# Moving the column sums and the spread of three norm passages to the last two steps of the tile loop

## The reference

```python
def rmsnorm_2(x, w):
    xf = x.astype(jnp.float32)
    y = xf * lax.rsqrt(jnp.mean(xf * xf, axis=-1, keepdims=True) + EPS)
    return (y * w.astype(jnp.float32)).astype(x.dtype)
...
        x = x + rmsnorm_2(y, norm_mix_post[layer])
        h = rmsnorm_2(x, norm_ffn_pre[layer])
        y = conv_ffn(h, ffn_w_up[layer], ffn_conv_w[layer], ffn_conv_b[layer], ffn_w_down[layer])
        x = x + rmsnorm_2(y, norm_ffn_post[layer])
        if layer == N_A_LAYERS - 1:
            k_sh, v_sh, c_sh = shared_kv(x, kv_norm, kv_w, kv_b_f)
```

## Time and profile before

| | |
|---|---|
| median of three runs | 2106.36 us (2105.05 to 2107.86) |
| time of the profiled execution | 2106.26 us |
| span in its profile | 2104.5 us |
| PE busy | 2046.5 us, 97% of the span |
| DVE busy | 1227.9 us, 58% |
| ACT busy | 791.7 us, 38% |
| mean granted clock of TensorE | 0.991 |

### The profile page before, as it was taken

One profiled execution on the slowest core, in us unless ns is written; L12 is line 12 of the kernel. 1 busy time (PEld: TensorE's weight loads), 2 busy tenths in 40 slices (PEclk: granted clock), 3 DMA queues, 4 the chain that ended last, 5 costly groups with the idle time before them and its releaser, 6 DMA issues.

```text
span 2104.5 us, 25495 instructions
## 1 busy us (share of the span) xinstructions
PE 2046.5 (97%) x9840; PEld 1658.8 (79%) x9848; DVE 1227.9 (58%) x1726; ACT 791.7 (38%) x1228; POOL 24.4 (1%) x45
## 2 busy tenths in 40 slices
PE   8999999999999999999899999999999999999997
PEld 6866778888888888877788888878786678888886
DVE  5778635454435355456675573774537767647475
ACT  4258243332222232245443342342426734324242
POOL 1000000000000000000000000000000000000000
PEclk9999999999999999999999999999999999999998
DMA  5410412322222222321122222222221022222221
GB/s 190 161 41 9 144 39 100 110 100 100 98 85 98 100 100 89 111 91 49 72 100 100 88 92 100 85 95 90 97 86 38 15 87 80 100 100 100 98 85 58
DMA packets 34320, 188.52 MB, mean 90 GB/s; under 512 B 4392, under 2 KB 8648, under 8 KB 14608
## 3 DMA queue, kind: packets, MB, share of 16 engines
q1 hardware_dynamic: 32448, 181.24, 24.2%
q0 software_dynamic: 1568, 5.65, 1.0%
q10 hardware_dynamic: 208, 0.33, 0.1%
HBM read 182.54 MB, written 2.11 MB: 88 GB/s over the span
## 4 chain that ended last, share of the span: by engine, by line
PE 86%; DVE 6%; PEld 3%; issue 2%; ACT 2%; DVEq 1%; PEldq 0%; DMA 0%; SPq 0%; ACTq 0%
PE bank L427 23%; PE bank L429 23%; PE bank L428 23%; PE bank L510 3%; PE bank L515 3%; PE bank L511 3%; PE bank L1242 2%; PE bank L1212 1%; PE bank L1229 1%; PEld bank L427 1%; PEld bank L429 1%; PEld bank L428 1%; PE bank L2250 1%; DVE xT L903 1%; DVE a_lo L688 1%
## 5 line engine op out<-in xcount | busy, mean ns | idle before, releaser
L356 ACT ACTIVATE w_hi<-w_raw 128x2048 fp32r<-128x2048 f32 (+3 forms) x168 | 307.7, 1832 | 760.6 <-PE bank L429 626.5
L427 PE MATMUL bank<-a_hi,w_hi 128*128 128x512 f32 x1376 | 538.6, 391 | 1.6 <-DVE w_lo L371 1.1
L429 PE MATMUL bank<-a_hi,w_lo 128*128 128x512 f32 x1376 | 535.6, 389 | 0.0
L428 PE MATMUL bank<-a_lo,w_hi 128*128 128x512 f32 x1376 | 535.5, 389 | 0.0
L371 DVE TENSOR_TENSOR w_lo<-w_raw,w_hi 128x2048 fp32r<-128x2048 f32 (+3 forms) x168 | 367.9, 2190 | 155.0 <-ACT w_hi L356 155.0
L427 PEld LDWEIGHTS bank<-a_hi,w_hi 128*128 128x128 f32 x1376 | 258.3, 188 | 56.5 <-issue 1.9
L429 PEld LDWEIGHTS bank<-a_hi,w_lo 128*128 128x128 f32 x1376 | 258.3, 188 | 53.8
L428 PEld LDWEIGHTS bank<-a_lo,w_hi 128*128 128x128 f32 x1376 | 258.4, 188 | 52.9
L427 PE MATMUL bank<-big_halves,w_hi 128*128 128x512 f32 x616 | 240.1, 390 | 0.5 <-DVE w_lo L371 0.3
L429 PE MATMUL bank<-big_halves,w_lo 128*128 128x512 f32 x616 | 239.7, 389 | 0.0
L428 PE MATMUL bank<-big_halves,w_hi 128*128 128x512 f32 x616 | 239.7, 389 | 0.0
(11 more groups left out here) (350 smaller groups left out, 2436.2 us busy)
## 6 DMA issues: line engine op xcount, KB each, us to landing
w_raw<-in_w_fu SPq DMA_DIRECT2D x44, 1024.0 KB, 4.8
w_raw<-in_w_up SPq DMA_DIRECT2D x16, 1024.0 KB, 4.8
w_raw<-in_w_down SPq DMA_DIRECT2D x16, 1024.0 KB, 4.8
w_raw<-in_w_fd SPq DMA_DIRECT2D x16, 1024.0 KB, 4.8
w_raw<-in_w_fd SPq DMA_DIRECT2D x8, 768.0 KB, 4.2
w_raw<-in_w_rqk SPq DMA_DIRECT2D x4, 1024.0 KB, 5.2
w_raw<-in_w_rvg SPq DMA_DIRECT2D x4, 1024.0 KB, 4.8
w_raw<-in_w_gate SPq DMA_DIRECT2D x4, 1024.0 KB, 4.8
```

Source lines behind the costliest of these rows:

```text
L356: act.activation(dst[0][:, cols], raw[slot][:, cols], ACT.Copy).then_inc(hi_half_ready.sem if half == 0 else hi_ready.sem, 1)
L427: pe.matmul(out, w[0], x[0], start=first, stop=False)
L428: pe.matmul(out, w[0], x[1], start=False, stop=False)
L429: return pe.matmul(out, w[1], x[0], start=False, stop=last)
```

## The change

The column sums stand after the eighth step instead of the sixth, and the spread after the ninth instead of the seventh. The instructions and their number are the same, and so are the instructions of the other engines and their order.

```diff
             def with_tile(pe, k):
-                if k == 5:
+                if k == 7:
                     pe.wait_ge(gathered.sem, b_ga + KT - 1)
                     column_sums(pe, 4, total, True, True).then_inc(sums_ready.sem, 1)
-                elif k == 6:
+                elif k == 8:
                     pe_root(pe)
```

## The result

The changed kernel takes 2116.2 us (median of five, 2115.4 to 2117.7) against 2106.4 us before (five, 2103.8 to 2107.9). The ratio is 1.0050, with a 95% interval of 1.0036 to 1.0064. That is 9.8 us slower by the medians; the forecast said 4.7.

A forecast was written before the change was run, and what follows sets the result against it. The prediction took PE as the bound, losing time where it waits or runs slower. Passage terms -0.85, +1.33 and +1.31 gave +1.8 us, two clock falls +2.9, so 2106.3 + 4.7 = 2111.0 us, range 2107.0 to 2113.6.

The forecast's parts named there:

- The wait at the sums: PE's wait for DVE's last additions before the column sums goes, returning 1.84, 0.98 and 1.25 us, 4.07 in all.
- the root's way: From sums to spread, root and reciprocal stay hidden under 2.37 us of sums and ninth step, with 0.77 us to spare.
- the third block waits for the first evacuation: With the spread last before it, PE's third block begins 3.22 us after the spread's start; PE stands 2.4 us.
- 11.04: Forecast time in us from the end of the sixth step to the third block, each passage, at full clock.
- the fourth block: In the feed-forward passages it waits 0.31 us more for the low weights that DVE splits.
- The terms of the second and the third passage: Net cost at full clock: +1.33 us in the second, +1.31 in the third including the fourth block's weight wait.
- the term of -0.85 us for the first passage: Net gain at full clock: 11.04 us against 12.20 now, -1.16, plus 0.31 for the fourth block's weights.
- the chance of a fall: Chance that the clock falls after each new wait: about 0.7; two falls taken, some 2.9 us.
- Case B: Rival: the clock falls behind the new wait in all three passages, 6.3 us slower, 2112.6 us; chance 0.22.
- C: Rival: third block waits, but the clock falls in one passage or none, 2108.1 to 2109.6 us; chance 0.28.
- D: Rival: the third block doesn't pay, the new wait much shorter than worked out; 2100.5 or 2105.8 us; chance 0.05.
- E: Rival: root's way not covered, ACT or DVE answering later; up to 0.6 us a passage, up to 2114.4; chance 0.03.

The follow-up runs named there:

- second profiles: Both kernels profiled and timed once more with no edit: the kernel before 2106.3 us, ratio 1.0001; the changed kernel 2115.4 us, ratio 1.0044.
- filled run: Changed kernel with nine more matmuls of 512 columns behind each spread, into a bank that nothing reads: 2113.4 us, ratio 1.0033 to the kernel before.
- second profile of before: The kernel before, profiled and timed once more with no edit: 2106.3 us, ratio 1.0001.

## Why the forecast was wrong

**Right: the mechanism and its place.** The wait at the sums went; the root's way is hidden; the third block waits for the first evacuation. 10.97 to 10.99 us from the sixth step in all three passages against 11.04; a wait of 2.2 us against 2.0 to 2.5; the fourth block 0.5 us late at full clock against 0.3. The terms of the second and the third passage, +1.33 and +1.31 us, came to 1.0 and 1.6 us in the second profiles (the stretch, and the fourth block's wait as in the filled run): 2.6 together, as forecast.

**Wrong, the step that failed most: the term of -0.85 us for the first passage.** It compared 11.04 with 12.20 us, of which 1.7 were a fall of the clock that the second profile of before hasn't. There the first passage's stretch is 27.0 us, as in the others, and the change costs it 1.2 us, with the fourth block's wait 1.7: the term was 2.6 us too low. The forecast noted the fall and counted its going as a gain. That the total of that execution matched the median was luck: a fall at 145 us and part of the slow stretch ahead of the first passage, both in the second profile, are missing from it.

**Wrong: the chance of a fall.** 0.7 a passage, two of three, 2.9 us. It was six of six in two profiles, and three falls cost 4.0 us by the comparison with the filled run (5.2 with the fourth block's wait in it). Case B, all three falls at 2112.6, was the better one. Its price for the falls, 4.5 us, was high enough; it was short by the term above and the one below.

**Missing: the clock ahead of a passage.** The forecast put it at nothing. Ahead of the second passage it fell 3 us earlier relative to the work, 1.2 us in the second profile; with the other entries and what lies ahead of the first one that is 0.9 us. The forecast also measured from the end of the sixth step, and so could not see what its +1.3 us a passage are made of. The old wait at the sums took up the slow first steps: the stretch is 27.0 us with 4 to 5 us of slow clock in them and 27.1 with none. The new order pays for them: 28.1 us with them, 26.8 without, so that with a full clock there the stretch would even have gained a little over 27.0.

With the terms set right the account is 3.16 + 5.17 + 1.40 - 0.53 = 9.20 us for the second profiles, against 9.8 by the medians of the first measurement and 9.2 by those of the second. The forecast's 4.7 lacks 4.5 of these 9.2: rounded, 2.6 us in the first passage's term, 1.1 in the falls and 0.9 ahead of the passages.

Of the rivals, C (the clock stays) fell; D fell with the waits of 2.2 us; E fell: the reciprocal was ready 0.9 us before the spread. The Trainium skill's section on psum-queue depth-cycling ("TensorE: Matmul & The Clock Gate") was named in the forecast, where it was said to put, taken strictly, a fall in every passage. The changed kernel agrees with it, six of six. The runs with the same wait of 2.2 us and one fall of three, and none of three, show that it is no rule for such a wait.

**Still open** is what decides whether a wait of 2.2 us brings a fall. Not its length alone, and not the distance of the sums. In the nine passages of the changed kernel and of the run with the sums behind the seventh step, the fall began 23.9 us after the slow stretch ahead of the passage had ended, and the third block 23.3 to 24.0 us after it. In the two passages with the spread alone moved that had no fall, the third block began 24.4 and 25.0 us after it, and in the one that had, 23.6. With TensorE kept busy ahead of the changed kernel's passages it was 28.7 us in the first, and in the other two no slow stretch lay ahead. So the moment seems to count, but no run shifts it alone, and this stays argued.

## What to carry to other kernels

A result that several evacuations need must come while there is still enough independent work behind it. Here 3.3 us pass from the spread's start to the next block: with twelve matmuls behind the spread TensorE didn't wait, with six it waited 0.8 us and with none 2.2. A wait is worth its length only if nothing slow ahead of it hides in it: before taking one away, look at what would then set the pace, the clock included. And one profile whose total equals the median may still hold a clock's fall in the very place that matters; compare a second one before counting it in a term.

## What the runs showed of the hardware

The falls of the granted clock are not scattered evenly. In code that no experiment up to there changed, a fall begins between 144.4 and 145.7 us in eight of the thirteen profiles and between 139.4 and 143.8 us in four more, and a slow stretch ahead of the first passage, 3.4 to 10.2 us long, begins between 1028.4 and 1029.7 us in nine. So a change that shifts the work by a microsecond or two shifts it against these falls, and that is of the size of what such a change is worth: 1.2 us at the second passage's entry here. The kernel before lost 8 us when TensorE was only kept busy in its waits; that moved falls cost these too is argued from the mean clock.
